# Plain fp32 products for a mixture of experts' slots, gates in the selection matrix, two more slab buffers, and a mean square per chunk

## The reference

```python
def grouped_moe(x, router_w, router_bias, w_gate_up, w_down):
    t = x.reshape(-1, D)
    scores = jax.nn.sigmoid((t @ router_w).astype(jnp.float32))
    ...                       # best group of 4 experts, then the best 2 in it: top_idx
    sel = jnp.take_along_axis(scores, top_idx, -1)
    weights = sel / jnp.sum(sel, -1, keepdims=True)
    gates = jnp.sum(jax.nn.one_hot(top_idx, N_EXPERTS, dtype=jnp.float32) * weights[..., None], 1)
    h = jnp.einsum('td,edf->tef', t, w_gate_up)
    a = jax.nn.silu(h[..., :D_EXPERT]) * h[..., D_EXPERT:] * gates[..., None].astype(h.dtype)
    y = jnp.einsum('tef,efd->td', a, w_down)
```

```python
h = h + 0.5 * swiglu(rms_norm_2(h, ffn1_norm[l]), ffn1_w1[l], ffn1_w3[l], ffn1_w2[l])
h = h + token_mixer(rms_norm_2(h, mix_norm[l]), w_in[l], ...)
h = h + 0.5 * swiglu(rms_norm_2(h, ffn2_norm[l]), ffn2_w1[l], ffn2_w3[l], ffn2_w2[l])
```

## Time and profile before

| | us |
|---|---|
| runs of the kernel: median (lowest to highest, 3 runs) | 1567.66 (1567.39 to 1568.59) |
| profiled execution: device time | 1570.28 |
| profiled execution: span, first to last instruction | 1568.5 |
| PE busy | 1537.0 (98%) |
| DVE busy | 834.4 (53%) |
| ACT busy | 706.1 (45%) |

### The profile page before, as it was taken

The page is one execution under the profiler, slowest core; times in us unless marked ns, Lnnn a source line. Parts: engine busy times, 40 slices in busy tenths (PEclk is TensorE's granted clock), DMA queues, the critical chain, the costliest instruction groups (busy, mean ns, idle before and its releaser), DMA issues.

```text
span 1568.5 us, 20466 instructions
## 1 busy us (share of the span) xinstructions
PE 1537.0 (98%) x7540; PEld 1175.6 (75%) x7540; DVE 834.4 (53%) x1114; ACT 706.1 (45%) x1147; POOL 88.6 (6%) x158
## 2 busy tenths in 40 slices
PE   8999999999999999999999999999999999999998
PEld 7876444877544588888888888888888888888886
DVE  4665215476422745556567555555555656755554
ACT  5662112683212434445374544454444546554443
POOL 2320000050000000000100000000000020000000
PEclk9999999999999999999999999999999999999999
DMA  7536997545699555556535656546555652655551
GB/s 243 201 119 261 409 412 279 168 167 211 277 416 413 200 190 183 187 193 203 161 109 187 197 187 193 186 146 212 189 187 179 208 185 87 221 188 184 187 190 57
DMA packets 165986, 328.31 MB, mean 209 GB/s; under 512 B 8874, under 2 KB 106896, under 8 KB 152992
## 3 DMA queue, kind: packets, MB, share of 16 engines
q1 hardware_dynamic: 164992, 323.52, 59.5%
q0 software_dynamic: 928, 3.89, 0.8%
HBM read 326.33 MB, written 1.05 MB: 209 GB/s over the span
## 4 chain that ended last, share of the span: by engine, by line
PE 92%; DVE 2%; ACT 2%; DMA 1%; issue 1%; DVEq 0%; POOL 0%; SPq 0%; POOLq 0%; ACTq 0%
PE bank L439 23%; PE bank L441 23%; PE bank L440 23%; PE bank L1198 7%; PE bank L1246 3%; PE bank L833 1%; PE bank L1158 1%; PE bank L1159 1%; PE bank L1254 1%; PE bank L862 1%; PE bank L1255 1%; DMA sb_xT<-exp_w_down 1%; PE bank L910 1%; DMA sb_raw<-w_in 1%; DVE sb_wlo L435 1%
## 5 line engine op out<-in xcount | busy, mean ns | idle before, releaser
L435 DVE TENSOR_TENSOR sb_wlo<-sb_raw,sb_whi 128x1024 fp32r<-128x1024 f32 (+2 forms) x419 | 483.3, 1197 | 345.3 <-ACT sb_whi L428 341.2
L428 ACT ACTIVATE sb_whi<-sb_raw 128x1024 fp32r<-128x1024 f32 (+2 forms) x419 | 407.9, 1027 | 318.5 <-PE bank L441 307.3
L439 PE MATMUL bank<-sb_whi,sb_op_hi 128*128 128x512 f32 (+2 forms) x1216 | 476.9, 392 | 6.4 <-DVE sb_op_lo L1982 3.5
L441 PE MATMUL bank<-sb_whi,sb_op_lo 128*128 128x512 f32 (+2 forms) x1216 | 469.2, 386 | 0.0
L440 PE MATMUL bank<-sb_wlo,sb_op_hi 128*128 128x512 f32 (+2 forms) x1216 | 468.5, 385 | 0.0
L439 PEld LDWEIGHTS bank<-sb_whi,sb_op_hi 128*128 128x128 f32 x1216 | 229.7, 189 | 53.5 <-issue 4.3
L441 PEld LDWEIGHTS bank<-sb_whi,sb_op_lo 128*128 128x128 f32 x1216 | 229.4, 189 | 46.4
L440 PEld LDWEIGHTS bank<-sb_wlo,sb_op_hi 128*128 128x128 f32 x1216 | 229.9, 189 | 43.0
L439 PE MATMUL bank<-sb_whi,sb_lat_hi 128*128 128x512 f32 (+2 forms) x456 | 175.7, 385 | 1.0 <-DVE sb_wlo L435 1.0
L441 PE MATMUL bank<-sb_whi,sb_lat_lo 128*128 128x512 f32 (+2 forms) x456 | 174.5, 383 | 0.0
L440 PE MATMUL bank<-sb_wlo,sb_lat_hi 128*128 128x512 f32 (+2 forms) x456 | 174.4, 382 | 0.0
(11 more groups left out here) (260 smaller groups left out, 1332.5 us busy)
## 6 DMA issues: line engine op xcount, KB each, us to landing
sb_raw<-ffn_w SPq DMA_DIRECT2D x264, 512.0 KB, 4.3
sb_moe<-exp_w_gate_up SPq DMA_DIRECT2D x50, 1024.0 KB, 8.6
sb_raw<-w_in SPq DMA_DIRECT2D x84, 512.0 KB, 4.7
sb_moe<-exp_w_down SPq DMA_DIRECT2D x26, 1024.0 KB, 8.6
sb_raw<-w_out SPq DMA_DIRECT2D x32, 512.0 KB, 4.2
sb_per_block<-exp_w_gate_up SPq DMA_DIRECT2D x8, 1024.0 KB, 7.8
sb_xT<-exp_w_gate_up SPq DMA_DIRECT2D x6, 1024.0 KB, 9.3
sb_xT<-exp_w_down SPq DMA_DIRECT2D x4, 1024.0 KB, 11.1
```

The source lines that it names most:

```text
L428: nc.scalar.activation(h, r, ACT.Copy).then_inc(hi_made.sem, 1)
L435: nc.vector.tensor_tensor(o, r, h.bitcast(F32), ALU.subtract).then_inc(lo_made.sem, 1)
L439: nc.tensor.matmul(ps, hi, wh, start=first, stop=False)
L441: return nc.tensor.matmul(ps, lo, wh, start=False, stop=last)
```

## The change

Gathers and scatters become one plain fp32 matmul each, and with them the hi and lo copies of x and of the pair's output go. The matmuls that bring the gates to slot order go too: instead DVE multiplies `in_slot` by the gates in place, after the gathers of that half have read it (`gated`), so that the turned matrix carries them. The output is copied once, its first half by ACT and its second by DVE. The slab buffers become 13. In the second block's first unit (first layer) each chunk gets its own mean square and power, ACT squares chunk 0 before it handles chunk 1, and one weight slab's split (`hi2(l, 2)`, `lo2(l, 2)`) is put earlier.

```diff
-MOE_RING = 3 * RING + 2
-RAW_SLOT, WHI_SLOT, WLO_SLOT, BLOCK_SLOT, XT_SLOT = (4, 5, 10), (6, 8, 0), (7, 9, 1), 2, 3
+MOE_RING = 3 * RING + 4
+RAW_SLOT, WHI_SLOT, WLO_SLOT = (9, 10, 5), (11, 1, 7), (12, 2, 8)
+BLOCK_SLOT, XT_SLOT, FREE_SLOT = 0, 6, (3, 4)
...
+        free = [sb(f"moe{3 * RING + i}", [P, SLAB]) for i in range(2)]
+        in_slot = sb("in_slot", [P, NC, NE, CAP])
+        pair_y = [y_out[:, p % 4, :] for p in range(PAIRS)]
...
+                for slot in FREE_SLOT:
+                    number = slab_number(0, S1, l, S1_OUT)
+                    expert_slab(slot, lambda: sp.wait_ge(slab_done.sem, number + (1 + RING)))
...
                 def gather(half, k, b, ch):
-                    nc.tensor.matmul(b[:, :], xs_hi[:, ch, k, :], to, start=ch == 0, stop=False)
-                    return nc.tensor.matmul(b[:, :], xs_lo[:, ch, k, :], to, start=False, stop=ch == 1)
+                    return nc.tensor.matmul(b[:, :], of_slab(x[:, ch, :], k), to, start=ch == 0, stop=ch == 1)
...
                 def pair_slots(p):
...
                     for ch in range(NC):
-                        nc.tensor.transpose(bank[5][:, ch * P:ch * P + P], to[ch], ident)
-                    for ch in range(NC):
-                        i = nc.tensor.matmul(bank[5][:, T:T + 2], to[ch], gates[:, ch, 2 * p:2 * p + 2], start=ch == 0, stop=ch == 1)
+                        i = nc.tensor.transpose(bank[5][:, ch * P:ch * P + P], to[ch], ident)
...
                 def scatter(p, ch, nh):
-                    wait(F, "y_lo", l, 2 * p + nh + 1)
-                    hi, lo = (y[:, 512 * nh:512 * nh + 512] for y in pair_y[p])
-                    to = of_slot[p][:, ch * P:ch * P + P]
-                    nc.tensor.matmul(ybank(ch, nh)[:, :], to, hi, start=False, stop=False)
-                    i = nc.tensor.matmul(ybank(ch, nh)[:, :], to, lo, start=False, stop=p == PAIRS - 1)
+                    wait(F, "of_slot", l, p + 1)
+                    wait(F, ("y_a", "y_d")[nh], l, p + 1)
+                    i = nc.tensor.matmul(ybank(ch, nh)[:, :], of_slot[p][:, ch * P:ch * P + P], pair_y[p][:, 512 * nh:512 * nh + 512],
+                                         start=False, stop=p == PAIRS - 1)
...
+                def gated(half):
+                    dve.drain()
+                    for ch in range(NC):
+                        v = in_slot[:, ch, 8 * half:8 * half + 8, :]
+                        tt(v, v, gates[:, ch, 8 * half:8 * half + 8].unsqueeze(2).to_broadcast([P, 8, CAP]), ALU.mult).then_inc(F["in_gated"].sem, 1)
+
+                gated(0)
...
+                        if h == 1:
+                            nc.scalar.activation(proj[:, ch, GA:GA + D], x[:, ch, :], ACT.Square, accum_out=ss_raw2[:, ch:ch + 1]).then_inc(G["ss_raw"].sem, 1)
+                        if n == 1:
+                            moe_done(act, DEPTH, last_use(WHI_SLOT[2]), 1)
+                            hi2(l, 2)
+                    act.wait_ge(first_rstd.sem, 1)
...
-                units_hi(G, l, BASE2, S2, 0, NU2, 0, column)
+                units_hi(G, l, BASE2, S2, 0, NU2, 0, column, second=lambda: wait(G, "rstd", l, 1))
```

More of the change, by code:

```diff
@@ L210, in program @@
         x = sb("x", [P, NC, D])
[L211 to L214, removed]
+        with ExitStack() as operands:
+            op_hi, op_lo, lat_hi, lat_lo = (operands.enter_context(nc.sbuf_tensor("sb_" + name, [P, n, T], F32R))
+                                            for name, n in (("op_hi", DK), ("op_lo", DK), ("lat_hi", 5), ("lat_lo", 5)))
+        y_out, places = sb("y_out", [P, 4, D]), sb("places", [P, 10, T])
         act_hi, act_lo = lat_hi[:, 0:2, :], lat_lo[:, 0:2, :]
@@ L241, in program @@
         xT = sb("xT", [P, DK, T])
[L242 to L247, removed]
+        free = [sb(f"moe{3 * RING + i}", [P, SLAB]) for i in range(2)]
+        in_slot = sb("in_slot", [P, NC, NE, CAP])
+        pair_y = [y_out[:, p % 4, :] for p in range(PAIRS)]
         xg = sb("xg", [P, 2, DK, 8 * CAP])
-        of_slot = [lat_hi[:, p, :] if p < 5 else lat_lo[:, p - 5, :] for p in range(PAIRS)]
+        of_slot = [places[:, p, :] for p in range(PAIRS)]
         xg_flat = xg[:, :, :, :].rearrange("p h k n -> p (h k n)")
         moe = [None] * MOE_RING
-        for slots, own in ((RAW_SLOT, slabs[0:3]), (WHI_SLOT, slabs[3:6]), (WLO_SLOT, slabs[6:9])):
+        for slots, own in ((RAW_SLOT, slabs[0:3]), (WHI_SLOT, slabs[3:6]), (WLO_SLOT, slabs[6:9]), (FREE_SLOT, free)):
             for i, t in zip(slots, own):
@@ L1203, in pair_slots @@
                 def pair_slots(p):
[L1204 to L1210, removed]
+                    to = [in_slot[:, ch, 2 * p:2 * p + 2, :].rearrange("p e n -> p (e n)") for ch in range(NC)]
+                    if p % 4 == 0:
+                        wait(F, "in_gated", l, p // 2 + 2)
+                    if p in (2, 3):
                         wait(F, "xg_d", l, 5 + 2 * p)
+                    elif p:
+                        wait(F, "of_slot", l, p)
                     for ch in range(NC):
[L1213 to L1215 removed]
+                        i = nc.tensor.transpose(bank[5][:, ch * P:ch * P + P], to[ch], ident)
                     i.then_inc(F["slot"].sem, 1)
@@ L1241, in pair_down @@
                         if p:
-                            wait(F, "y_lo", l, 2 * p - 1 + nh)
+                            wait(F, ("y_a", "y_d")[nh], l, p)
                         for f in range(2):
@@ L1553, in units_hi @@
                 ahead(j0 + 3, 0)
+                second()
                 silu(0, num(j0 + 1), (1,))
@@ L1738, in products_done, with down_out @@
                     moe_done(act, l, up_slab(p, 1) + 1)
[L1740 to L1747, removed]
+                def down_out(p):
+                    wait(F, "y0_a", l, p + 1)
+                    wait(F, "y0_b", l, p + 1)
+                    nc.scalar.activation(pair_y[p][:, 0:512], bank[6][:, :], ACT.Copy).then_inc(F["y_a"].sem, 1)
                 with act.If(size > CAP):
@@ L1772, in _ @@
                         wait(F, "slot", l, p + 1)
-                        for e, r in enumerate((slice(0, CAP), slice(CAP, P))):
-                            nc.scalar.activation(slot_gates[r, p:p + 1], bank[5][r, T + e:T + e + 1], ACT.Copy)
                         nc.scalar.activation(of_slot[p], bank[5][:, 0:T], ACT.Copy).then_inc(F["of_slot"].sem, 1)
[L1776 to L1781, removed]
+                        if p == PAIRS - 1:
+                            following(1, (0,))
+                        if p:
+                            down_out(p - 1)
+                    following(1, (1,))
+                    down_out(PAIRS - 1)
             for l in range(DEPTH):
@@ L2303, in _ @@
                     following(1, (1,))
-                    for nh in range(2):
-                        down_lo(PAIRS - 1, nh)
+                    down_out(PAIRS - 1)
                 def next_lo(h):
```

83 lines of the change are left out of this document (37 added, 46 removed).

## The result

The changed kernel took 1610.45 us (median of 4 runs, 1609.6 to 1611.0) where before took 1568.12 beside it: a ratio of 1.0271, 95% interval 1.0258 to 1.0284. That is slower by 42.3 us.

What follows compares the result with a forecast made beforehand. PE was taken as the bound (98% busy), with transfers close behind in the expert stage. +51.6 - 5.4 - 0.2 - 1.0 - 4.8 = +40.2 us on 1567.66 gave 1607.9 us; 8 in 10 for 1601 to 1616.

Steps and rivals of the forecast that it cites:

- the narrower range: Whole kernel: the forecast's own range of 1603 to 1612 us, with a 75% chance.
- The plain product: Gathers and scatters: each plain product adds 0.403 us over its pair, 128 of them, +51.6 us, all on PE's path.
- The wait for `y_lo`: Scatters near the end of a layer's experts: their wait goes, 0.1 us a layer, -0.2 us.
- The step of four: Gathers' weight loads: x is read with a step of four numbers; taken as costing nothing.
- The bound of 0.21 to 0.24 us for the load's pace: Gathers' weight loads: pace of 0.11 us becomes 0.21 to 0.24 with the step, under the 0.43 us record.
- The rival of visible loads: Gathers: a load outlasts the record before it, 0.13 us shown on each of 128 records, +16.6 us, 1624.5; 8%.
- Four passes: Plain products: true fp32 as exactly four passes through the array would make the term 58.2 us; rows decided for 51.6.
- The gates' matmuls: After the transposes in each of 16 pairs: 0.34 us goes, -5.4 us; DVE's multiplications instead are hidden.
- Thirteen slabs: Second layer's last slab: PE's wait of 1.01 us goes, -1.0 us; it would go even with eleven buffers.
- The sign that I had named: Profile after: expert stages some 23 us longer each, with a DMA share under 1.
- The first unit: Second block's first unit, first layer: gap of 1.94 us goes (-1.9) and the lower clock behind it (-2.9), -4.8 us.
- The rival that the clock falls all the same: Second block's first unit: the clock still falls because the zero matmuls are little work, +2.9 us, 1610.8; 8%.

Runs made afterwards that it cites:

- kernel 4: The changed kernel with the gathers' stationary operand read with a step of one number instead of four (output order differs): 1609.21 us.
- kernel 7: The kernel before, with the tokens' high and low parts kept in token order and read with a step of four by float32r gathers: 1571.27 us, ratio 1.0027.
- kernel 6: The kernel before with the second block's first unit changed and the gates' products replaced by a sum on ACT, float32r pairs kept: 1561.83 us, ratio 0.9968.
- kernel 3: The changed kernel with eleven slab buffers in the ring of weights instead of thirteen: 1610.08 us, ratio 1.0267 to before.
- kernel 2: The kernel before with two unused products of 128x512 put in PE's wait ahead of the second block's first unit, first layer: 1566.51 us, ratio 0.9988.
- Kernel 1: The kernel before with only the edit of the second block's first unit, all products still float32r pairs: 1564.49 us, ratio 0.9978.

## Why the prediction held, point by point

The time forecast was 1607.9, the median came to 1610.45, inside the narrower range too; the sum of +40.2 stands against +40.6 in the spans.

- **The plain product, +51.6.** The reading that decided it, two records for each plain product, is shown: 128 records for 64 matmuls, twice. The term was some 1.7 us too high. By the chain the scatters cost 12.52 us a layer, where it had 32 x 0.403 = 12.9, and the gathers 13.26, of which the step has 0.83 (29.44 us in the chain, 28.61 in kernel 4), so 12.43: 49.9 us for both kinds and layers. The pair that I had priced at 0.455 us takes 0.46 or more, since a group's first record is longer in the chain of before (0.43 us behind `pair_down`, 0.50 behind a wait, 0.34 and 0.47 in pair 0) and the others in it take up to 0.25.
- **The wait for `y_lo`, -0.2.** It is within the scatters' 12.52 us: before, one of their records waited for DVE's lo (264.14, 0.41 us where its neighbours took 0.23), 0.2 us in this layer where I had put 0.1.
- **The step of four, taken as nothing.** It costs 1.7 us (kernel 4), at group starts, which I had overlooked: in all groups but the one behind scatters the first load starts with the group's first product or at most 0.1 us before it, so nothing hides it. The bound of 0.21 to 0.24 us for the load's pace was not contradicted: loads start 0.235 us apart in kernel 7. These 1.7 us and the 1.7 too much in the term of the products cancel, by luck, which is why the stages came out at +23.01 and +21.99 beside the forecast's 23.0 and 22.0. The sum was better than its terms.
- **The rival of visible loads** (a load outlasts the record before it) could not be judged by the record of 311 ns. Loads that start 0.235 us apart are well within the 0.43 us of a plain product's record, and the rival's +16.6 us did not come; beside float32r products (0.227 us) they are just past the point, and cost 0.008 us on each. Where the Trainium skill (SBUF — State Buffer, Door 1) speaks for slower reads with such a step, the traces agree in sign (311 ns against 190), and in time it was worth 1.7 us here.
- **Four passes.** The Trainium skill (FP8 and Floating Point Precision, TensorE Precision Notes) counts four for true fp32; exactly four would have made the plain products 6.6 us dearer than the forecast's term. The rows of after stay at 3.43 us for four products, 3.8 times the 0.2274 of a float32r one.
- **The gates' matmuls, -5.4.** The `L1215` rows are gone, and pair 5 to the next is 14.78 us, as worked out (14.8). The new multiplications on DVE stand nowhere in the chain, but their cover was thinner than I wrote: DVE's copies of the gathers stand before them and came later with the dearer gathers, so in the first layer they end at 162.41 us and not near 155.4, 2.5 us before PE wants them (164.87). But the term is worth 5.4 only beside dear products: in kernel 6, where the transfers are the next bound, it is worth 3.9.
- **Thirteen slabs, -1.0.** The wait of 1.01 us went, and kernel 3 shows that the buffers had no part in it. The sign that I had named, a DMA share under 1 in the expert stages, came. Over the first layer's pairs, before and then after:

```profile
160.00:260.00 100.00, 99.44 (x469) 41.55 (x469) 26.74 (x42) 20.07 (x46) 0.00 (x0) 1.00 1.01 409
```

```profile
160.00:260.00 100.00, 99.44 (x394) 38.40 (x391) 18.60 (x32) 7.59 (x19) 0.00 (x0) 1.00 0.90 360
```

  The share fell from 1.01 to 0.90 (0.91 in kernel 3). A short stretch misleads here: 230 to 240 us still has 1.02, 200 to 210 us has 0.78. So the transfers no longer run all the time, and no slab is late. The wait isn't fixed between executions either: kernel 2, with before's expert stage, had a second stage of 126.74 us with no such wait, and one of 0.21 us in its first.
- **The first unit, -4.8.** 1.92 and 2.86, against 1.94 and 2.9. Kernel 1 shows the two together, kernel 2 the clock apart. The rival that the clock falls all the same is out.

The median stands 2.1 us more above before's than the forecast's sum says, and 1.7 more than the spans differ. That is how the profiled executions lie in their sets: before's (1570.28) is 2.2 us above its median, after's (1611.0) 0.6 above its own. Which part of the change those 1.7 us belong to, if any, is not shown.

## What to carry to other kernels

Before an exact fp32 product takes the place of a float32r hi and lo pair, count records against matmuls in the order of the program: here one plain product of 128x512 was two records of 0.43 us, 0.858, against 0.46 for the pair, and what the splitting saved on ACT and DVE was off the path. Separate the parts of a mixed change: some 10 us of good edits (4.8 for the first unit, 5.4 for the gates' matmuls) lay under 50 us of a bad one. Before a sign is called wrong or right by a busy share, take it over the whole stage. A short wait on PE can cost more in clock behind it than in itself, and a few unused products in it are a cheap first test.

## What the runs showed of the hardware that I had not expected

- A weight load's record is longer than its pace. With a step of four numbers it lasts 0.31 us, yet loads start 0.235 us apart and overlap in the records; with a step of one it lasts 0.188 to 0.190.
- A gap of 1.94 us on PE at full clock was followed by the granted clock at 0.50, 1.2 GHz, for long enough to cost 2.86 us; 1.91 us of unused products in the same gap kept it at 1.00.
- 0.12 us more for a load shows once for a group of gathers whose first load starts with its product or at most 0.1 us before: behind a wait (143.73 and 143.74 us in the kernel after), behind transposes (164.97 and 165.07), and behind `pair_down` (both at 181.75). It does not show for the group behind scatters (1.72 us in both kernels), where the load starts at 202.82 and the product at 203.24.
